# The second layer's modulation moves from setup into the first retrieval, and GpSimd's level differences move ahead of its weight splits

## What is computed

```python
def _adaln(cvec, w, b):
    mod = jax.nn.silu(cvec) @ w + b
    return jnp.split(mod, 6, axis=-1)

for l in range(DEPTH):                      # DEPTH = 2
    sh1, sc1, g1, sh2, sc2, g2 = _adaln(c, ada_w[l], ada_b[l])   # ada_w[l]: 1024 x 6144
    x = x + g1 * mixer_l(_modulate(_rms_norm(x, norm1_w[l]), sh1, sc1))
    x = x + g2 * _peer(_modulate(_rms_norm(x, norm2_w[l]), sh2, sc2))

def _peer(h, w_q, sub_keys, u_tab, v_tab):
    q = (h @ w_q).reshape(tokens, 8, 2, 128)                # 8 heads, two halves
    s = jnp.einsum('thpk,hpnk->thpn', q, sub_keys)          # 128 keys a half
    s_top, i_top = lax.top_k(s, 16)
    comb = s_top[:, :, 0, :, None] + s_top[:, :, 1, None, :]
    c_top, c_pos = lax.top_k(comb, 16)
    ...
```

## Time and profile before

| | |
|---|---|
| median of 3 executions | 4578.3 us (4576.36 to 4580.62) |
| the profiled execution | 4575.59 us, span 4573.8 us |
| busy: TensorE, VectorE, ScalarE, GpSimd | 4120.9, 3779.5, 1645.1, 1992.2 us |
| mean granted TensorE clock | 0.942 of 2.4 GHz |
| setup | 0 to about 160 us of the span |
| HGRN2 mixer and first output projection | to about 848 us |
| first retrieval | to about 1049 us |

### The profile page before, as it was taken

The page is one execution under the profiler, slowest core; times in us unless marked ns, Lnnn a source line. Parts: engine busy times, 40 slices in busy tenths (PEclk is TensorE's granted clock), DMA queues, the critical chain, the costliest instruction groups (busy, mean ns, idle before and its releaser), DMA issues. The chain is left out here.

```text
span 4573.8 us, 72999 instructions
## 1 busy us (share of the span) xinstructions
PE 4120.9 (90%) x24791; PEld 3718.7 (81%) x24791; DVE 3779.5 (83%) x6714; ACT 1645.1 (36%) x2312; POOL 1992.2 (44%) x1435
## 2 busy tenths in 40 slices
PE   7888987976899999999996887886899999999997
PEld 3588887875799999999996876884779999999996
DVE  7677776599888888999996887488978888899997
ACT  7544443213333333333334443221433333333333
POOL 3233323214555454565653221320745444556663
PEclk9899997988999999999998888987999999999998
DMA  9411111213999999999982110220899999999995
GB/s 371 157 40 55 47 38 70 65 37 81 288 365 361 364 364 356 364 361 364 363 333 68 54 38 22 83 72 11 183 339 361 364 361 362 359 363 363 360 363 209
DMA packets 616028, 1049.50 MB, mean 229 GB/s; under 512 B 229699, under 2 KB 388870, under 8 KB 615430
## 3 DMA queue, kind: packets, MB, share of 16 engines
q1 hardware_dynamic: 467814, 508.86, 32.8%
q0 software_dynamic: 147456, 536.94, 31.6%
q10 hardware_dynamic: 672, 2.62, 0.1%
HBM read 982.75 MB, written 65.54 MB: 229 GB/s over the span
## 5 line engine op out<-in xcount | busy, mean ns | idle before, releaser
L1924 POOL DMA_INDIRECT rows_ex<-in_peer_v,ctx_index x512 | 707.1, 1381 | 476.1 <-DVE row_acc_ex L1999 360.5
L1924 POOL DMA_INDIRECT rows_ex<-in_peer_u,ctx_index x512 | 586.9, 1146 | 628.6 <-DVE dots_ex L2002 500.1
L2085 PE MATMUL pu_ex<-h_hi,uT_hi_ex 128*128 128x384 f32 x2048 | 715.3, 349 | 1.9 <-ACT coef_ex L1949 1.0
L1999 DVE SCALAR_TENSOR_TENSOR row_acc_ex<-rows_ex,factor_ex,row_acc_ex 128x1024 f32<-128x1024 f32 x512 | 657.6, 1284 | 52.8 <-issue 11.2
L2085 PE MATMUL pu_ex<-h_lo,uT_hi_ex 128*128 128x384 f32 x2048 | 692.3, 338 | 0.0
L2085 PE MATMUL pu_ex<-h_hi,uT_lo_ex 128*128 128x384 f32 x2048 | 692.2, 338 | 0.0
L2093 PE MATMUL py_ex<-v_hi_ex,c_hi_ex 128*128 128x512 f32 x1536 | 622.5, 405 | 0.0
L2002 DVE CUSTOM_DVE_ANT_0 rows_ex<-rows_ex,h_row_ex 128x1024 f32<-128x1024 f32 x512 | 604.2, 1216 | 0.0
L2093 PE MATMUL py_ex<-v_lo_ex,c_hi_ex 128*128 128x512 f32 x1536 | 601.0, 391 | 0.0
L2093 PE MATMUL py_ex<-v_hi_ex,c_lo_ex 128*128 128x512 f32 x1536 | 600.6, 391 | 0.0
L1990 DVE TENSOR_TENSOR uT_lo_ex<-pT_ex,uT_hi_ex 128x512 fp32r<-128x512 f32 x512 | 351.5, 686 | 176.0 <-ACT uT_hi_ex L1938 152.3
(11 more groups left out here) (434 smaller groups left out, 8535.6 us busy)
## 6 DMA issues: line engine op xcount, KB each, us to landing
u_raw_ex<-in_peer_u SPq DMA_DIRECT2D x256, 512.0 KB
v_raw_ex<-in_peer_v SPq DMA_DIRECT2D x256, 512.0 KB
ada<-in_ada_w SPq DMA_DIRECT2D x24, 2048.0 KB, 9.8
gates<-stage_ro SPq DMA_DIRECT2D x12, 4096.0 KB, 16.0
g_raw_ex<-gates SPq DMA_DIRECT2D x256, 192.0 KB
w_raw_hgrn<-in_hgrn_w_in SPq DMA_DIRECT2D x40, 512.0 KB
w_raw_re<-in_peer_w_q SPq DMA_DIRECT2D x32, 512.0 KB, 3.7
w_raw_gla<-in_gla_w_in SPq DMA_DIRECT2D x25, 512.0 KB
```

The source lines that it names most:

```text
L1924: pool.indirect_dma_start(out=rows[m % RING][:, :], out_offset=None, in_=a["peer_u" if m < TG * NC else "peer_v"].rearrange("l n d -> (l n ...
L1999: nc.vector.scalar_tensor_tensor(row_acc[g][:, :], rows[j][:, :], factor[:, j:j + 1], row_acc[g][:, :], ALU.mult, ALU.add).then_inc(row_fr ...
L2085: last_ = nc.tensor.matmul(pu[:, 0:TD], w[:, k, :], x[:, k, 0:TD], start=(k == 0 and w is uT_hi[b] and x is h_hi), stop=(k == DC - 1 and w ...
```

## The change

Three things.

1. `setup` makes the modulation of layer 0 only: 12 blocks instead of 24.
2. `retrieve` of layer 0 makes that of layer 1, in 16 blocks of 384 columns, one for each half of a head. SyncE loads a block (1.5 MB), ScalarE makes its high part, GpSimd its low part (3072 elements a partition; in setup VectorE made it), TensorE has 16 matmuls of 384 columns behind the scores of that half, ScalarE copies the row, TensorE turns it (3 products) between the two halves of a later projection, ScalarE copies the turned row, and VectorE adds all biases at the end. Raw, high and low parts have two buffers each. `retrieve` of layer 1 has none of that.
3. In both mixers GpSimd's three levels come one behind the other, ahead of the low part of chunk 2, which stood between levels 0 and 1.

```diff
-    NALL = DEPTH * NBL
+    NALL = NBL
...
                 for l in range(POOL_LEVELS):
                     exponents(pool.tensor_tensor, l)
                     pool.drain().then_inc(pool_diff, 1)
-                    if l == 0 and (2 < L or not final):
-                        lo(h, 2)
-                for j in range(3, NCH):
+                for j in range(2, NCH):
                     if j < L or not final:
                         lo(h, j)
...
+                    if later:
+                        sp.wait_ge(ada_lo_done, h * 2 + (b + 1))
+                        sp.dma_start(ada[b][:, :, :], ada_w[:, :, bass.ds(h * (2 * AW) + b * AW, AW)]) \
+                            .then_inc(ada_in[b], 16)
...
+            def ada_low(h, b):
+                if later:
+                    pool.wait_ge(ada_hi_done, h * 2 + (b + 1))
+                    pool.tensor_tensor(ada_lo[b][:, :, :], ada[b][:, :, :], ada_hi[b][:, :, :].bitcast(F32),
+                                       ALU.subtract).then_inc(ada_lo_done, 1)
+
+            low(0, 0)
+            low(0, 1)
+            with pool.Fori(0, PH - 1) as h:
                 for b in range(2):
...
+                    ada_low(h, b)
+                    low(h + 1, b)
+            ada_low(PH - 1, 0)
+            ada_low(PH - 1, 1)
...
+            with act.Fori(1, PH - 1) as h:
                 for b in range(2):
+                    row(h - 1, b)
+                    ada_high(h, b)
+                    turned_copy(h - 1, b)
                     copies(h, b)
                     hi(h + 1, b)
...
-            def project(h, b):
+            def project(h, b, turns=True):
...
                 for i, cols in halves():
+                    if i == 1 and turns:
+                        turn_row(h - 1, b)
...
+            def modulation(h, b):
+
+                if later:
+                    pe.wait_ge(ada_lo_done, h * 2 + (2 + b + 1))
+                    if not (isinstance(h, int) and h == 0 and b == 0):
+                        pe.wait_ge(mod_done, h * 2 + b)
+                    for w, part in enumerate((ada_hi[b], ada_lo[b])):
+                        for k in range(DC):
+                            last = nc.tensor.matmul(pm[0:4, 0:AW], c["cs4"][:, k, :], part[:, k, :],
+                                                    start=(w == 0 and k == 0), stop=(w == 1 and k == DC - 1))
+                    last.then_inc(ada_mm, 1)
...
+            def after(h, b):
+                scores(h, b)
+                modulation(h, b)
+
+            project(0, 1, False)
+            after(0, 0)
+            with pe.Fori(1, PH) as h:
+                project(h, 0)
+                after(h - 1, 1)
                 project(h, 1)
-                scores(h, 0)
-                project(h + 1, 0)
-                scores(h, 1)
-            project(PH - 1, 1)
-            scores(PH - 1, 0)
-            scores(PH - 1, 1)
+                after(h, 0)
+            turn_row(PH - 1, 0)
+            after(PH - 1, 1)
+            turn_row(PH - 1, 1)
```

More of the change, by code:

```diff
@@ L1427, in retrieve, with turned_row @@
         dve_passed = sem("dve_passed")
+        later = layer + 1 < DEPTH
+        AW = 6 * D // (2 * PH)
+        if later:
+            ada_w = a["ada_w"][layer + 1].rearrange("(k p) n -> p k n", p=P)
+            ada = [sb(f"ada{i}", [P, DC, AW]) for i in range(2)]
+            ada_hi = [sb(f"ada_hi{i}", [P, DC, AW], F32R) for i in range(2)]
+            ada_lo = [sb(f"ada_lo{i}", [P, DC, AW], F32R) for i in range(2)]
+            mod_row = sb("mod_row", [P, AW])
+            mod_raw = sb("mod_raw", [P, 48, 2])
+            pm = ps("pm", [P, 512])
+            ada_in = [sem(f"ada_in{i}") for i in range(2)]
+            ada_hi_done, ada_lo_done, ada_mm, row_out, row_turned, mod_done = (sem(n) for n in
+                ("ada_hi_done", "ada_lo_done", "ada_mm", "row_out", "row_turned", "mod_done"))
+        def turned_row():
+            return pm[:, AW:AW + 2 * AW // P].rearrange("p (i v) -> p i v", v=2)
         nm = Norm(nc, c, h_hi, h_lo, layer, 1, sem, y, pS[0][:, 0, 0:NT], pS[1][:, 0:4, :], pS[1][:, 4, :])
@@ L1444, in _, with low @@
             pool.sem_inc(w_lo_done, 2)
[L1445 removed]
+            if later:
+                pool.sem_inc(ada_lo_done, 2)
+            def low(h, b):
+                pool.wait_ge(w_hi_done, h * 2 + (b + 1))
+                pool.tensor_tensor(w_lo[b][:, :, :], w_raw[b][:, :, :], w_hi[b][:, :, :].bitcast(F32),
+                                   ALU.subtract).then_inc(w_lo_done, 1)
+            def ada_low(h, b):
+                if later:
+                    pool.wait_ge(ada_hi_done, h * 2 + (b + 1))
[4 more added lines that the diff above has]
+            with pool.Fori(0, PH - 1) as h:
                 for b in range(2):
[L1447 to L1449 removed]
+                    ada_low(h, b)
+                    low(h + 1, b)
+            ada_low(PH - 1, 0)
+            ada_low(PH - 1, 1)
         @block.scalar
@@ L1468, in copies, with ada_high, row, turned_copy @@
                     act.activation(qT[b][:, cols], pq[i][:, 0:HALF], ACT.Copy).then_inc(q_out, 1)
+            def ada_high(h, b):
+                if later:
+                    act.wait_ge(ada_in[b], h * 16 + 16)
+                    act.activation(ada_hi[b][:, :, :], ada[b][:, :, :], ACT.Copy).then_inc(ada_hi_done, 1)
+            def row(h, b):
+                if later:
+                    act.wait_ge(ada_mm, h * 2 + (b + 1))
+                    act.activation(mod_row[0:4, :], pm[0:4, 0:AW], ACT.Copy).then_inc(row_out, 1)
+            def turned_copy(h, b):
+                if later:
+                    act.wait_ge(row_turned, h * 2 + (b + 1))
+                    n = AW // P
+                    act.activation(mod_raw[:, bass.ds(h * (2 * n) + b * n, n), :], turned_row(), ACT.Copy).then_inc(mod_done, 1)
             nm.root(act)
@@ L1475, in _ @@
                     hi(0, 1)
-            with act.Fori(0, PH - 1) as h:
+            for b in range(2):
+                ada_high(0, b)
+                copies(0, b)
+                hi(1, b)
+            with act.Fori(1, PH - 1) as h:
                 for b in range(2):
+                    row(h - 1, b)
+                    ada_high(h, b)
+                    turned_copy(h - 1, b)
                     copies(h, b)
                     hi(h + 1, b)
-            copies(PH - 1, 0)
-            copies(PH - 1, 1)
+            for b in range(2):
+                row(PH - 2, b)
+                ada_high(PH - 1, b)
+                turned_copy(PH - 2, b)
+                copies(PH - 1, b)
+            for b in range(2):
+                row(PH - 1, b)
+                turned_copy(PH - 1, b)
         @block.tensor
@@ L1513, in _, with turn_row @@
             first_product(nc, pe, nm, pq, w_hi[0], w_lo[0], proj)
-            with pe.Fori(0, PH - 1) as h:
-                project(h, 1)
-                scores(h, 0)
-                project(h + 1, 0)
-                scores(h, 1)
-            project(PH - 1, 1)
-            scores(PH - 1, 0)
-            scores(PH - 1, 1)
+            def modulation(h, b):
+                if later:
+                    pe.wait_ge(ada_lo_done, h * 2 + (2 + b + 1))
[6 more added lines that the diff above has]
+                    last.then_inc(ada_mm, 1)
+            def turn_row(h, b):
+                if later:
+                    pe.wait_ge(row_out, h * 2 + (b + 1))
+                    for i in range(AW // P):
+                        last = nc.tensor.matmul(turned_row()[:, i, :], mod_row[0:4, i * P:(i + 1) * P], c["fold"][0:4, :],
+                                                start=True, stop=True)
+                    last.then_inc(row_turned, 1)
+            def after(h, b):
[6 more added lines that the diff above has]
+                after(h - 1, 1)
+                project(h, 1)
+                after(h, 0)
+            turn_row(PH - 1, 0)
+            after(PH - 1, 1)
+            turn_row(PH - 1, 1)
         @block.vector
@@ L1561, in _ @@
                                       cpos[:, :, :])
+            if later:
+                dve.wait_ge(mod_done, 2 * PH)
+                bias = c["vec"][:, VEC["ada_b"] + 48 * (layer + 1):VEC["ada_b"] + 48 * (layer + 2)]
+                nc.vector.tensor_tensor(c["mod"][:, layer + 1, :, :], mod_raw[:, :, :],
+                                        bias.unsqueeze(2).to_broadcast([P, 48, 2]), ALU.add)
+                dve.drain()
 def route(nc, c, chosen, gates_dram, ctx_index, ctx_gate, layer):
```

6 lines of the change are left out of this document (3 added, 3 removed).

## The result

| | us, median | profiled execution's span |
|---|---|---|
| before | 4577.64 (4576.36 to 4580.62) | 4573.8 |
| after | 4547.05 (4544.84 to 4549.11) | 4542.9 |

The account below looks back on a forecast made before the run. No engine was taken to bound all: TensorE and VectorE waited for each other in the HGRN2 mixer, VectorE bound the first retrieval. Terms −64.8 + 29.4 − 26 − 3 = −64.4 gave 4514 us, range 4496 to 4546.

Parts of the forecast that it names:

- Setup, −64.8: Setup: losing modulation blocks 12 to 23 saves 64.8 us, the last row being copied out at about 92.8 us.
- First retrieval, +29.4: First retrieval: sixteen added modulation blocks make TensorE the bound at 11.77 us a unit; +29.4 us, +21.2 without the hold.
- The hold: First retrieval: VectorE's first candidate sum waits for the end of GpSimd's 6.9 us subtraction; sums end after 17.0 us, not 8.8.
- the rule of whole instructions: VectorE and GpSimd: two such instructions exclude each other as wholes, in alternation, rather than sharing element by element.
- First mixer, −26: HGRN2 mixer: three levels ahead of chunk 2's low part gain 4.0 us a head, 24 for six, 2 for head 0.
- both halves of the term: HGRN2 head: 1.5 us from VectorE's earlier factors plus 2.5 us from TensorE avoiding the low clock, 4.0 in all.
- Second mixer, −3: GLA mixer: TensorE's 2.24 us wait becomes about 1.4, VectorE is held 1 us less in three heads; −3 (0 to −9).
- the sentence under "Sum": Whole kernel: −64.8 + 29.4 − 26 − 3 = −64.4 us, so 4511.2, and 4513.9 as a median.
- my rivals: Mixers give little (chance 0.27), no hold in the retrieval (0.12), slower than before (0.05), setup saves less (0.03).
- rival 1: Mixers: the new order gives nothing or little, −10 instead of −26 (4530 us) or +6 (4546); chance 0.27.
- 4514: Whole kernel: the forecast median in us after the change.

Follow-up runs that it names:

- e9: e8 with SyncE asking in the first retrieval for both halves' query weights and keys first, ada's columns behind them; 4514.9 us, ratio 0.9865.
- e10: e8 with GpSimd's low part of ada in four instructions of 128x768 in place of one of 128x3072; 4515.1 us, ratio 0.9864.
- e11: e8 with half of the modulation's sum left out, 8 matrix products in place of 16 a unit of the first retrieval; 4502.7 us, ratio 0.9836.
- e14: The kernel before with GpSimd's new order in the first mixer alone; 4552.9 us, ratio 0.9941.
- e13: The kernel before with GpSimd's new order in the second mixer alone; 4578.4 us, ratio 1.0001.
- e1: The changed kernel with an unused constant of 96 bytes a partition behind fold; 4524.0 us, ratio 0.9882.
- e2: The kernel before with an unused constant of 160 bytes a partition and nothing else; 4601.6 us, ratio 1.0053.
- e5: The changed kernel with 96 unused bytes ahead of stage, in the routing alone; 4527.0 us, ratio 0.9887.
- e8: e1 with GpSimd's old order in the second mixer; 4518.6 us, ratio 0.987.
- e12: e8 with 192 unused bytes ahead of u_raw in the experts' stage, so both weight streams begin at a multiple of 256; 4513.8 us, ratio 0.986.

## Why the prediction was wrong

**Setup, −64.8: right.** The last block's row, ScalarE:

```profile
93.14 0.59 ACT L355 ACTIVATE mod_row<-pa 4x512 f32<-4x512 f32 x1 [4.49 <-PE pa L393]
```

93.14 for 157.53 is −64.4. By the table's border, GpSimd's first level difference, it is −63.5.

**First retrieval, +29.4: right, +31.0 by the table.** TensorE:

```profile
795.72 0.82 PE L1597 MATMUL pm_re<-fold,mod_row_re 4*128 4x2 f32 x6 [2.01 <-ACT mod_row_re L1514]
...
812.09 1.28 PE L1571 MATMUL pS_re<-kT_re,qT_re 128*128 128x128 f32 x10
813.12 1.63 PE L1589 MATMUL pm_re<-ada_hi_re,cs 128*4 128x384 f32 x8
814.58 1.55 PE L1589 MATMUL pm_re<-ada_lo_re,cs 128*4 128x384 f32 x8
```

The modulation costs 3.0 us (I had 2.77) and the turn 0.82 (0.73); batches of scores come each 11.98 us (11.77), and TensorE waits for VectorE nowhere. The 2.0 us wait in the first row was not in my working: ScalarE stood for the first `w_raw` behind `ada` on the queue, which e9 mends. The hold is there:

```profile
808.17 6.78 DVE L1645 TENSOR_TENSOR cand_re<-top_re 128x320 f32<-128x320 f32 x3
```

That is the first head, 6.8 us for the 0.76 of the earlier trace rows. Its end is GpSimd's: the subtraction of 6.81 us beside it began at 807.54 and ended at 814.35. The hold comes in every head but the last and becomes shorter as VectorE falls behind, which my working had right: the sums take 5.9 us in the second head and 3.8 in the third to sixth, where the end of the long subtraction and the short one for the query weights behind it share the holding. That fits the rule of whole instructions, and e10 shows it at another size; e11 shows that it doesn't set the unit.

**First mixer, −26: right.** The table has −30.0, e14 alone −25.3. GpSimd's level 0, and TensorE in two heads:

```profile
280.36 0.73 POOL L618 TENSOR_TENSOR ex_hgrn<-b_hgrn 128x320 f32<-128x320 f32 x1 [15.24 <-DVEq L928]
...
343.81 0.73 POOL L618 TENSOR_TENSOR ex_hgrn<-b_hgrn 128x320 f32<-128x320 f32 x1 [15.24 <-DVEq L928]
```

```profile
295.26 0.41 PE L496 MATMUL pp_hgrn<-h_hi,w_hi_hgrn 128*128 128x320 f32 x1 [2.59 <-POOL w_lo_hgrn L683]
...
368.10 1.31 PE L1118 MATMUL pA_hgrn<-ident,t_hgrn 128*128 128x128 f32 x10 [1.72 <-DVEq L985]
```

A head takes 63.45 us, where the earlier trace rows have 68.1. The one stop of 6.81 us became one of 2.6 to 3.0 for the low part (I had 3.05), and a second of 0.6 to 2.1 (I had 1 to 2). The gain is 4.7 us a head (I had 4.0). In the window 368.10 to 372.00 the granted clock is 1.00, the full of the two levels (2.4 GHz), where the earlier trace rows have 0.50: both halves of the term as it was worked out.

**Second mixer, −3: wrong, if small.** e13's median puts it at 0 (within 4 us), and the stages at +2 to +4 with the two behind it (see e13).

That the edited stages sum to −62.5 for a forecast of −61.4 is in part luck: setup gave 1.3 less than its term, the first mixer 4.0 more, and the retrieval cost 1.6 more.

**The step that failed** is the sentence under "Sum": I added up stages that the diff edits and took all others to stay as they were. The tiles that move into the constants stood in the diff, and I gave them no term. The stages behind the retrieval lost 31.6 us. Placement is 23 (e1) to 25 (e2) of them, 20 of it the stores of the gates (e5), the rest in the stages of the experts. That is the term I had put at nothing. What is left of the 31.6, 5 to 8 us, fits the new order in the second mixer and the new code in the second retrieval (below). None of my rivals was this one; the measured time lies 1 us above rival 1's upper end, but its mechanism, mixers that give nothing, is not what happened.

**Open.** The second retrieval with the output projection ahead of it is longer with the new code of the retrieval, whatever the order in the mixer: with the old order 283.3 to 284.0 us for 280.8 to 281.7 (e11 alone has 281.9), with the new one 284.4 to 286.0 for 282.8. So that code costs 2 to 3 us there, though layer 1 makes no modulation. It has new pieces and its loop is cut at other places; which of that costs the time wasn't tried. With the placement mended e1's median is still 10 us above 4514, and its profile 15 us above the forecast for it: 3.5 in setup, 3 in the first retrieval (32.4 for 29.4), 4.5 in the second mixer's term, 4 in the second retrieval, 3 in the experts' stages, less 1 in the first mixer and 2 in the routings. Terms smaller than the 6.0 us between e1 and e8 in the same code are certain only where many profiles agree, as above.

## What to carry to other kernels

A tile that is added to, or moved among, long-lived ones shifts the address of everything allocated behind it, so look at where the targets and sources of transfers begin, above all of those in short pieces, and give them a multiple of 256 or round the constants up to one. When the expected gain is missing, line up the same instruction at the borders of the stages of both traces; a stage with unchanged code and another length points at placement or at the state that it is entered in. A transfer that hides under computation has a margin (here 14.5 us against 18.1). Past it, each costs what it outlasts the computation by (19.2 less 18.1), and only the last one, with nothing beside it, costs its full difference (19.2 less 14.5).

## What the runs showed of the hardware

- Stores read from SBUF in pieces of 256 bytes take a third longer on the wire when the pieces begin at an address that is no multiple of 256: 218 GB/s for 290, at 32, 128 and 160 bytes past the multiple alike. From issue to landing a store takes 23.2, 22.6 and 23.2 us there, for 16.0.
- The stages of the experts, which stream their weights in pieces of 4096 bytes, show little of it: some 3 us in stages of 1284 and 1236 when all their tiles lie 160 bytes on, and e12, which aligned the two streams from 64 past a multiple, could not tell that from nothing.
- The new order in the second mixer goes with a mean granted clock of 0.85 or 0.86 there, for 0.87, in all eighteen profiles.
- The four pieces of e10 were no cheaper for VectorE than one. A short VectorE instruction with two SBUF inputs waits for GpSimd's whole running one, 6.8 us for 0.8, and with four pieces in place of one each of three instructions in a row can wait for one (so in three of eight heads; 32.0 us in all for 31.5).
